# Even mixer of a ten-stage transformer kernel: C B products moved behind the x groups, output projection moved between scan units, bias mask made by matmul, products moved from GpSimd to VectorE

## The chip, the cores and the metric

The kernel runs on one core of one Trainium2 chip. The metric is the time of one execution on the device in microseconds. A core has TensorE (PE: matmuls, and the weight loads, PEld), VectorE (DVE), ScalarE (ACT), GpSimd (POOL) and SyncE (SP), each with a list of instructions of its own, run in order. They meet through semaphores. All constants, weights and inputs come from HBM by DMA.

## The reference, cut to what matters

x is 256 rows of 1024. It goes through ten stages: two macaron layers of feed-forward, mixer, feed-forward (stages a, conv, b, c, attn, d), then the even mixer, feed-forward e, the odd mixer and feed-forward f. Only the even mixer is touched:

```python
def even_mixer(x, ...):
    proj = rms_norm_2(x, mix_norm) @ w_in              # 1024 -> q, k, v (512 each), z (1024), xbc (2048), dt (32)
    q, k = rms_norm_2 of each head                     # 8 heads of 64
    na_out = neighbourhood_attention(q, k, v, rpb)     # 4 x 64 grid, window of 16 columns, relative bias
    xbc = silu(centred_depthwise_conv(xbc, conv_w, conv_b))   # 4 taps
    xs, bm, cm = split(xbc)                            # 1024, 512 (B), 512 (C)
    y = ssd_scan(forward) + ssd_scan(backward) + D_skip * xs  # 16 heads, 4 groups, chunks of 128
    ssd_out = gated_group_rms_norm(y, z, out_norm)
    return concatenate([na_out, ssd_out]) @ w_out      # 1536 -> 1024

# in neighbourhood_attention, for every row and head
s = q @ k * scale + bias[dy, dx]
s = where(in_win, s, -inf);  p = softmax(s);  o = p @ v

# in ssd_scan, for every chunk
y_diag = (C @ B^T * decay) @ (x * dt);   y_off = C @ h_prev * exp(a_cum)
```

## The kernel before, in words

The 256 rows are two tiles (t or l = 0, 1) of 128 partitions. Weights come as 260 pieces of 128 x 2048 f32, 1 MB each, in the order of use; SP loads them (`fetch`), ACT rounds a piece to f32r (`wh`, L1137), DVE makes the remainder (`wl`, L1752), and a product is three f32r matmuls: high by high, high by low, low by high. A loaded piece has 7 buffers (RAW), a rounded one 5 (RING). A piece p can only be rounded when p-5 has been used, and loaded when p-7 has been used. `ring.fill(most, done)` and `ring.need(upto)` in the lists of ACT and DVE say where in the list these splits stand. Both engines take them in order, so a split that waits for TensorE holds up everything behind it.

The even stage has 24 pieces, p0 = 160. On every engine its order is written out by hand as a list of calls, in `even()` of `tensor_program` (L835), `scalar_program` (L1440), `vector_program` (its `even`, with the list from L2259), `gpsimd_program` (L2466) and the load list in `sync_program`. The parts:

- `z_part`, then `group(0)` to `group(3)`: transposed projections of C, B and x. GROUPS = (2, 3, 0, 1), so groups 0 and 1 bring B and C, groups 2 and 3 bring x. ACT copies (`take`), DVE convolves (L2099), ACT applies silu (`gate`).
- `dt`: softplus on 64 columns over ACT and DVE (`steps_begin`, `step_exp`, `steps_middle`, `step_log`, `steps_end`); its result a2 (L2131) feeds `sums`, which yields the running sums and, through DVE's `sums`, the rows (L2145) for the decays.
- `state_products`: C B products of both tiles, banks 6, 7 and 2, 3.
- `qk_part`, `qk_turn`, `v_part`: q, k, v of the neighbourhood attention, with q's and k's norm: ACT squares, DVE `qk_sum`, POOL's root (L2439, L2442), DVE `qk_scale` (L2157, L2162, the latter makes qkg).
- the scan, in 8 units u of four heads (0 to 3 for tile 0): `decays(u)` builds the exponents of both directions in banks 2 and 3, ACT exponentiates (L1530), DVE `weigh(u)` multiplies (L2184), DVE `steps_x(u)` makes x dt (L2175), `outputs(u)` multiplies into banks 4 and 5. `crossing(l)` adds the state that crosses the chunks, from xe, which POOL's `entering(l)` makes (L2480). POOL's `skip` makes D x of tile 0 (L2489), DVE that of tile 1 (L2196). Then `skipped`, `gated` (L2207, L2210), ACT's `group_squares` (L1540), POOL's `group_root`, DVE's `normed` (L2219), and `turn_ssd` transposes the tile and splits it (L1547, L2226).
- the attention, in four pairs of heads i: SP's `nab_load(i)` (16 DMAs, L2588) brings the bias, reversed in each 64 columns; POOL's `nab_mask(i)` multiplies it by the window and adds -1e30 outside (L2503, L2505); TensorE `scores(i)`, DVE adds the bias (L2240) and takes the maximum (L2242), ACT exponentiates (L1555), DVE `divide(i)` (L2252), TensorE `turn(i, kk)` and `values(i)`.
- the output projection: pieces p0+18 to p0+21 for the scan (`out_ssd(q, t)`), p0+22 and p0+23 for the attention (`out_hood(q, t)`), 12 matmuls of 512 columns each, summed in banks 0 to 3. The `seam` adds it to x and scales for the next stage.

The whole output projection of tile 0 stands behind the last scan unit, `outputs(7)`.

## Time and profile before

| | before |
|---|---|
| median of 3 runs | 1761.22 us (1759.41 to 1762.1) |
| profiled execution | 1762.39 us, span 1761.1 us |
| PE busy | 1663.8 us, 94% |
| DVE busy | 981.4 us, 56% |
| ACT busy | 786.9 us, 45% |
| POOL busy | 100.2 us, 6% |
| mean granted TensorE clock | 0.968 |
| even stage, TensorE | about 1014 to 1261 us |

A row of a view of groups gives the line, the engine, the operation, what it writes and reads, the shapes and the count. In a view in order of time the first number is the start in us, the second the duration of the row (several instructions can be merged), and the bracket at the end the idle time before it with what ended it. PEclk is the granted clock in parts of 2.4 GHz. A busy PE is not PE at its peak: ends of matmuls are modelled, so unit costs are best taken between starts.

### The profile page before, as it was taken

The numbers are of one execution on the slowest core, as the hardware profiler recorded it, in microseconds if no ns is written. First come the engines' busy times: TensorE is split into PE (matmuls) and PEld (weight loads), VectorE is DVE, ScalarE is ACT, GpSimd is POOL, SyncE is SP. The second block draws the span as 40 slices with busy tenths as digits, with TensorE's granted clock in tenths as the row PEclk, the third lists the DMA queues.
The fourth block names the chain that finished last, engine by engine and source line by source line (L and its number), as shares of the span: only waits on it lengthen the run. The fifth ranks groups of instructions, "written<-read, shape, count | busy, mean of one in ns | idle before, by whom it ended". The sixth has DMA issues, their size and how long they took to land. (4 is left out here: it accounts for less than half of the span.)

```text
span 1761.1 us, 18639 instructions
## 1 busy us (share of the span) xinstructions
PE 1663.8 (94%) x7930; PEld 1357.7 (77%) x7930; DVE 981.4 (56%) x989; ACT 786.9 (45%) x953; POOL 100.2 (6%) x118
## 2 busy tenths in 40 slices
PE   6999998999999999989999998997899998599999
PEld 5877776788878888887888888775688886378887
DVE  4646675554474546665454556666545457644543
ACT  5444544444353434554343456433444444534442
POOL 1000100100010000001000000224000002000000
PEclk9999998999999999999999999977999999699999
DMA  8444541555455544543554453323365544025451
GB/s 325 186 185 174 191 156 48 193 189 191 169 190 193 200 184 178 197 166 120 191 195 187 176 194 122 119 61 88 127 220 186 191 185 153 1 96 218 188 191 48
DMA packets 51391, 289.36 MB, mean 164 GB/s; under 512 B 14023, under 2 KB 14791, under 8 KB 18026
## 3 DMA queue, kind: packets, MB, share of 16 engines
q1 hardware_dynamic: 50732, 286.87, 44.4%
q8 instruction: 63, 1.03, 0.2%
q10 hardware_dynamic: 576, 1.29, 0.2%
q14 instruction: 20, 0.16, 0.0%
HBM read 287.09 MB, written 1.05 MB: 164 GB/s over the span
## 5 line engine op out<-in xcount | busy, mean ns | idle before, releaser
L1752 DVE TENSOR_TENSOR wl<-raw,wh 128x2048 fp32r<-128x2048 f32 x260 | 588.8, 2286 | 177.9 <-ACT wh L1137 177.9
L513 PE MATMUL ps<-wh,xTh 128*128 128x512 f32 x1408 | 560.5, 398 | 20.1 <-DVE wl L1752 8.4
L513 PE MATMUL ps<-wh,xTl 128*128 128x512 f32 x1408 | 553.5, 393 | 0.0
L513 PE MATMUL ps<-wl,xTh 128*128 128x512 f32 x1408 | 553.2, 393 | 0.0
L1137 ACT ACTIVATE wh<-raw 128x2048 fp32r<-128x2048 f32 x260 | 489.0, 1907 | 2.7 <-PE ps L513 1.5
L513 PEld LDWEIGHTS ps<-wh,xTh 128*128 128x128 f32 x1408 | 267.6, 190 | 86.3 <-issue 10.1
L513 PEld LDWEIGHTS ps<-wh,xTl 128*128 128x128 f32 x1408 | 267.3, 190 | 57.3
L513 PEld LDWEIGHTS ps<-wl,xTh 128*128 128x128 f32 x1408 | 268.0, 190 | 54.1
L2439 POOL TENSOR_SCALAR st<-st 128x1 f32<-128x1 f32 (+2 forms) x46 | 30.3, 658 | 1452.7 <-ACT tmp L1156 850.5
L1200 ACT ACTIVATE sgf<-ps,st 128x256 f32<-128x256 f32 x22 | 10.5, 476 | 104.1 <-PE ps L513 104.1
L1200 ACT ACTIVATE sge<-ps,st 128x256 f32<-128x256 f32 x22 | 10.5, 476 | 99.5 <-PE ps L513 99.5
L513 PE MATMUL ps<-xTh,wh 128*128 128x256 f32 x192 | 54.7, 285 | 0.0
L513 PE MATMUL ps<-xTl,wh 128*128 128x256 f32 x192 | 54.3, 283 | 0.0
L513 PE MATMUL ps<-xTh,wl 128*128 128x256 f32 x192 | 54.3, 283 | 0.0
L1200 ACT ACTIVATE sgc<-ps,st 128x256 f32<-128x256 f32 x22 | 10.4, 474 | 96.0 <-PE ps L513 96.0
L1200 ACT ACTIVATE sgd<-ps,st 128x256 f32<-128x256 f32 x22 | 10.4, 475 | 95.6 <-PE ps L513 95.6
L1200 ACT ACTIVATE sgb<-ps,st 128x256 f32<-128x256 f32 x22 | 10.4, 474 | 93.0 <-PE ps L513 93.0
L1824 DVE SCALAR_TENSOR_TENSOR hbe<-ps,st,sge 128x256 f32<-128x256 f32 x22 | 10.6, 484 | 73.6 <-ACT sge L1200 73.5
L1824 DVE SCALAR_TENSOR_TENSOR hbf<-ps,st,sgf 128x256 f32<-128x256 f32 x22 | 10.6, 484 | 72.9 <-ACT sgf L1200 72.9
L1200 ACT ACTIVATE sga<-ps,st 128x256 f32<-128x256 f32 x22 | 10.5, 476 | 91.2 <-PE ps L513 91.2
L1824 DVE SCALAR_TENSOR_TENSOR hbc<-ps,st,sgc 128x256 f32<-128x256 f32 x22 | 10.6, 483 | 70.0 <-ACT sgc L1200 70.0
L1824 DVE SCALAR_TENSOR_TENSOR hbd<-ps,st,sgd 128x256 f32<-128x256 f32 x22 | 10.6, 483 | 69.7 <-ACT sgd L1200 69.7
(329 smaller groups left out, 2328.6 us busy)
## 6 DMA issues: line engine op xcount, KB each, us to landing
raw<-in_w SPq DMA_DIRECT2D x260, 1024.0 KB, 4.8
gains<-in_rows SPq DMA_DIRECT2D x18, 512.0 KB, 4.1
x<-in_x ACTq DMA_DIRECT2D x2, 512.0 KB, 8.4
qn<-in_rpb SPq DMA_DIRECT2D x32, 32.0 KB, 2.5
xd<-in_rpb SPq DMA_DIRECT2D x32, 32.0 KB, 2.6
out_x<-x SPq DMA_DIRECT2D x2, 512.0 KB, 2.6
df<-in_cst SPq DMA_DIRECT2D x1, 368.0 KB, 23.4
tri<-in_cst SPq DMA_DIRECT2D x1, 320.0 KB, 6.1
```

What stands on the lines that cost most here:

```text
L513: return pe.matmul(o, lhs, rhs, start=start, stop=stop, skip_group_check=False)
L1137: act.activation(wh[:, p % RING, :], raw[:, p % RAW, :], ACT.Copy).then_inc(*hi(p))
L1200: act.activation(r.sg[:, j % 2, t, :], bank(ffn_bank(j, t))[:, 0:256], ACT.Silu, scale=stat(("r", name, t))).then_inc(*silu(f, j, t))
L1752: TT(wl[:, p % RAW, :], raw[:, p % RAW, :], wh[:, p % RING, :].bitcast(F32), ALU.subtract).then_inc(*lo(p))
L1824: STT(r.hb[:, j % 2, t, :], bank(ffn_bank(j, t))[:, 256:512], stat(("r", name, t)), r.sg[:, j % 2, t, :], ALU.mult, ALU.mult).then_inc(*pr ...
L2439: pool.tensor_scalar(v, ss, mul, add, ALU.mult, ALU.add).then_inc(*mean(*name))
```

## The change

- Window mask: the constant `win` is only 0 or -1e30, ACT makes an f32r copy `winr`, and `scores` begins each bank with one matmul identity x winr of 512 columns, onto which q k is summed. DVE's addition reads the raw bias reversed. POOL's `nab_mask` is gone.
- Bias blocks: four semaphores; block 0 goes to qn, 1 and 2 to the two halves of nab, 3 to xd. nab_load(1) waits for decays(7), nab_load(3) for outputs(7), block 2 for nothing of its own. fetch(184) stands ahead of nab_load(0).
- `entering` and the skip product of tile 0 go from POOL to DVE.
- `sums` stands in the middle of `group(3)` (`mid`), not ahead of the products; `state_products` is split by tile, in banks 4, 5 and 2, 3, and stands behind group(3) and around qk_part(0, 0); the x turns and qk_turn(0, 0) come later, `crossing(0)` behind `outputs(0)`.
- `turn_ssd(0)` uses banks 6 and 7 and stands behind outputs(5); out_ssd(0..3, 0) stand between the units 7, the scores and the last outputs. turn(3, 1) uses bank 6. The tail's turns, values and out_hood are regrouped; out_hood(1, 0) stands inside out_ssd(3, 1).
- The lists of ACT and DVE follow, with many splits at other places.

```diff
@@ -855,15 +860,15 @@
         m.then_inc(*formed("sums"))
         emptied[2], emptied[3] = [(made, "dec")], [(made, "sums_lo")]
 
-    def state_products():
+    def state_products(t):
         on.wait_ge(silu, "xc", 3)
-        for t, b in ((0, 6), (1, 2)):
-            clear(b, b + 1)
-            for g in range(4):
-                m = mm(bank(b + g // 2)[:, 256 * (g % 2):256 * (g % 2) + 256], ev.xc[:, 8 + g, 128 * t:128 * t + 128],
-                       ev.xc[:, 12 + g, :], True, True)
-            m.then_inc(*formed("cb", t))
-            emptied[b] = emptied[b + 1] = [(copied, "cb", t)]
+        b = 2 if t else 4
+        clear(b, b + 1)
+        for g in range(4):
+            m = mm(bank(b + g // 2)[:, 256 * (g % 2):256 * (g % 2) + 256], ev.xc[:, 8 + g, 128 * t:128 * t + 128],
+                   ev.xc[:, 12 + g, :], True, True)
+        m.then_inc(*formed("cb", t))
+        emptied[b] = emptied[b + 1] = [(copied, "cb", t)]
 
     def qk_part(j, t):
         project("evenmix", p0 + 12 + 2 * j, t, 6 + t, (made, "qk", j, t))
...
@@ -923,30 +928,34 @@
 
     def turn_ssd(l):
         on.wait_ge(made, "ssd_out", l)
+        b0 = 2 if l else 6
         for b in range(2):
-            clear(2 + b)
-            transposes(2 + b, [xn[:, l, 512 * b + 128 * k:512 * b + 128 * k + 128] for k in range(4)]).then_inc(*flipped("ssd", l, b))
-            emptied[2 + b] = [(act_lo, "ssd", l, b)]
+            clear(b0 + b)
+            transposes(b0 + b, [xn[:, l, 512 * b + 128 * k:512 * b + 128 * k + 128] for k in range(4)]).then_inc(*flipped("ssd", l, b))
+            emptied[b0 + b] = [(act_lo, "ssd", l, b)]
 
     def scores(i):
         clear(6, 7)
         on.wait_ge(copied, "qk", 1, 1)
-        for t in range(2):
-            for hh in range(2):
-                u = slice(64 * hh, 64 * hh + 64)
-                m = mm(bank(6 + hh)[:, 256 * t:256 * t + 256], ev.qTn[u, i, 128 * t:128 * t + 128], ev.kTn[u, i, :], True, True)
+        on.wait_ge(copied, "win")
+        for hh in range(2):
+            mm(bank(6 + hh), ev.trir[:, 0, :], spread(ev.winr[:, :], 1, 8), True, False)
+            u = slice(64 * hh, 64 * hh + 64)
+            for t in range(2):
+                m = mm(bank(6 + hh)[:, 256 * t:256 * t + 256], ev.qTn[u, i, 128 * t:128 * t + 128], ev.kTn[u, i, :], False, t == 1)
         m.then_inc(*scored("hood", i))
         emptied[6] = emptied[7] = [(weighed, "hood", i, 1)]
 
     def turn(i, kk):
         on.wait_ge(made, "hood", i)
-        clear(4)
+        b = hood_bank(i, kk)
+        clear(b)
         for hh in range(2):
             for t in range(2):
-                m = pe.transpose(bank(4)[:, 256 * hh + 128 * t:256 * hh + 128 * t + 128],
+                m = pe.transpose(bank(b)[:, 256 * hh + 128 * t:256 * hh + 128 * t + 128],
                                  hood_P(i)[:, t, hh, 128 * kk:128 * kk + 128], ident[:, :])
         m.then_inc(*turned("hood", i, kk))
-        emptied[4] = [(copied, "hood", i, kk)]
+        emptied[b] = [(copied, "hood", i, kk)]
 
     def values(i):
         clear(5)
...
@@ -986,20 +995,20 @@
     emptied[3] = [(made, "dt")]
     group(1)
     group(2)
-    sums()
-    state_products()
-    group(3)
+    group(3, sums)
+    state_products(0)
     qk_part(0, 0)
+    state_products(1)
     x_turn(0)
     qk_part(0, 1)
+    x_turn(1)
     decays(0)
-    x_turn(1)
-    qk_turn(0, 0, 4)
+    qk_turn(0, 0, 5)
     qk_part(1, 0)
     decays(1)
     qk_turn(0, 1, 5)
+    outputs(0)
     crossing(0)
-    outputs(0)
     qk_part(1, 1)
     decays(2)
     outputs(1)
...
@@ -1016,38 +1025,37 @@
     outputs(4)
     decays(6)
     outputs(5)
+    turn_ssd(0)
+    out_ssd(0, 0)
     decays(7)
     outputs(6)
+    out_ssd(1, 0)
     scores(0)
     outputs(7)
-    turn_ssd(0)
-    out_ssd(0, 0)
+    out_ssd(2, 0)
     scores(1)
-    out_ssd(1, 0)
+    out_ssd(3, 0)
     turn(0, 0)
-    out_ssd(2, 0)
     turn(0, 1)
     scores(2)
-    out_ssd(3, 0)
     turn_ssd(1)
+    values(0)
     turn(1, 0)
-    values(0)
     out_ssd(0, 1)
     turn(1, 1)
     scores(3)
     out_ssd(1, 1)
+    values(1)
     turn(2, 0)
-    values(1)
+    turn(2, 1)
+    out_hood(0, 0)
+    values(2)
+    turn(3, 0)
+    turn(3, 1)
     out_ssd(2, 1)
-    turn(2, 1)
-    out_ssd(3, 1)
-    turn(3, 0)
-    values(2)
-    out_hood(0, 0)
-    turn(3, 1)
+    values(3)
+    out_ssd(3, 1, lambda: out_hood(1, 0))
     out_hood(0, 1)
-    values(3)
-    out_hood(1, 0)
     turn_in(AFTER["even"], 0)
     out_hood(1, 1)
 
...
     ring.need(p0 + 6)
@@ -1592,44 +1600,44 @@
     take(0, 1)
     gate(0, 0)
     ring.need(p0 + 8)
-    ring.fill(1, p0 + 6)
+    ring.fill(2, p0 + 6)
+    gate(0, 1)
     take(1, 0)
-    gate(0, 1)
-    step_exp()
-    ring.fill(1, p0 + 6)
     take(1, 1)
-    step_log()
     gate(1, 0)
     ring.need(p0 + 10)
     ring.fill(1, p0 + 8)
+    step_exp()
     take(2, 0)
+    step_log()
     gate(1, 1)
     ring.fill(1, p0 + 8)
     take(2, 1)
-    sums()
     gate(2, 0)
-    sum_rows()
-    state_products()
     ring.need(p0 + 12)
     ring.fill(1, p0 + 10)
+    gate(2, 1)
...
@@ -2166,6 +2173,11 @@
         TT(ev.dte[:, 1, :], d3[0][:, 0, 0:16], ev.dec[:, 2, :], ALU.mult)
         TT(ev.dte[:, 0, :], d3[0][:, 1, 16:32], ev.dec[:, 3, :], ALU.mult).then_inc(*made("dte"))
 
+    def entering(l):
+        on.wait_ge(copied, "xs", 1 - l, 1)
+        on.wait_ge(made, "dte")
+        TT(xe_of(l).rearrange("p (h d) -> p h d", d=64), heads(xn[:, 1 - l, :]), spread(ev.dte[:, l, :], 2, 64), ALU.mult).then_inc(*made("xe", l))
+
     def steps_x(u):
         l, q = u // 4, u % 4
         on.wait_ge(copied, "xs", l, q // 2)
...
@@ -2236,8 +2246,11 @@
             on.wait_ge(formed, "off", 1)
         for t in range(2):
             S = bank(6, 2).rearrange("p (h t n) -> p h t n", h=2, t=2)[:, :, t, :]
-            on.wait_ge(pooled, "nab", i, t)
-            TT(P[:, t, :, :], B[:, t, :, :], S, ALU.add).then_inc(*weighed("hood", i, t))
+            on.wait_ge(nab_in[i], i)
+            Bt = B[:, t, :, :]
+            rev = bass.AP(tensor=Bt.tensor, offset=Bt.offset + 63, ap=[list(Bt.ap[0]), [256, 2], [64, 4], [-1, 64]])
+            TT(P[:, t, :, :].rearrange("p h (j c) -> p h j c", c=64), rev, S.rearrange("p h (j c) -> p h j c", c=64),
+               ALU.add).then_inc(*weighed("hood", i, t))
             on.wait_ge(weighed, "hood", i, t)
             dve.tensor_reduce(ev.sm[:, a + 6 * t:a + 6 * t + 2], P[:, t, :, :], AX.X, ALU.max, negate=True).then_inc(*peaked("hood", i, t))
 
...
@@ -2264,63 +2277,63 @@
     turn_in("evenmix", 1)
     ring.fill(1, p0)
     key_gain()
-    ring.fill(1, p0 + 2)
-    ring.fill(1, p0 + 4)
+    ring.fill(2, p0 + 2)
     ring.need(p0 + 6)
     ring.fill(2, p0 + 4)
     convolve(0, 0)
-    ring.need(p0 + 8)
-    ring.fill(1, p0 + 6)
     convolve(0, 1)
     steps_begin()
-    ring.fill(1, p0 + 6)
+    ring.need(p0 + 8)
+    ring.fill(2, p0 + 6)
     convolve(1, 0)
-    steps_middle()
+    convolve(1, 1)
     ring.need(p0 + 10)
     ring.fill(1, p0 + 8)
-    convolve(1, 1)
+    steps_middle()
+    convolve(2, 0)
     steps_end()
     ring.fill(1, p0 + 8)
-    convolve(2, 0)
-    sums()
+    convolve(2, 1)
     ring.need(p0 + 12)
     ring.fill(1, p0 + 10)
-    convolve(2, 1)
+    convolve(3, 0)
+    sums()
     ring.fill(1, p0 + 10)
-    convolve(3, 0)
+    convolve(3, 1)
     ring.need(p0 + 14)
     ring.fill(1, p0 + 12)
-    convolve(3, 1)
     qk_sum(0, 0)
     factors()
     steps_x(0)
+    qk_scale(0, 0)
     ring.fill(1, p0 + 12)
-    qk_scale(0, 0)
     qk_sum(0, 1)
+    steps_x(1)
     weigh(0)
+    qk_scale(0, 1)
     ring.need(p0 + 16)
-    qk_scale(0, 1)
-    steps_x(1)
-    ring.fill(1, p0 + 12)
+    entering(0)
+    ring.fill(1, p0 + 13)
     qk_sum(1, 0)
     weigh(1)
     qk_scale(1, 0)
+    entering(1)
+    ring.fill(1, p0 + 14)
     crossed(0)
-    ring.fill(1, p0 + 14)
     steps_x(2)
     qk_sum(1, 1)
     weigh(2)
     ring.need(p0 + 18)
     qk_scale(1, 1)
-    ring.fill(1, p0 + 14)
+    ring.fill(1, p0 + 15)
     steps_x(3)
     weigh(3)
     ring.fill(1, p0 + 16)
+    skipped(0)
     steps_x(4)
-    skipped(0)
     weigh(4)
+    ring.fill(1, p0 + 17)
     gated(0)
-    ring.fill(1, p0 + 16)
     crossed(1)
     steps_x(5)
     weigh(5)
...
@@ -2328,14 +2341,13 @@
     steps_x(6)
     weigh(6)
     ring.fill(1, p0 + 18)
+    turn_ssd(0)
     steps_x(7)
     weigh(7)
     ring.need(p0 + 22)
+    scores(0)
     skipped(1)
-    turn_ssd(0)
     gated(1)
-    scores(0)
-    ring.fill(1, p0 + 18)
     scores(1)
     divide(0)
     normed(1)
...
@@ -2473,53 +2485,16 @@
         on.wait_ge(peaked, "qk", j, t)
         root(("qk", j, t), stat(("ss", "qk", j, t), 8), mul, add, 8)
 
-    def entering(l):
-        on.wait_ge(copied, "xs", 1 - l, 1)
-        on.wait_ge(made, "dte")
-        on.wait_ge(formed, "cb", 1)
-        pool.tensor_tensor(xe_of(l).rearrange("p (h d) -> p h d", d=64), xn[:, 1 - l, :].rearrange("p (h d) -> p h d", d=64),
-                           spread(ev.dte[:, l, :], 2, 64), ALU.mult).then_inc(*pooled("xe", l))
-
-    def skip():
-        Dk = small[:, SMALL["dskip"][0]:SMALL["dskip"][0] + 16]
-        x3 = xn[:, 0, :].rearrange("p (h d) -> p h d", d=64)
-        on.wait_ge(made, "xd", 3)
-        on.wait_ge(pooled, "xe", 1)
-        on.wait_ge(small_in_)
-        pool.tensor_tensor(x3, x3, spread(Dk, 2, 64), ALU.mult).then_inc(*pooled("xk"))
-
-    def nab_mask(i):
-        raw_in = hood_raw(i)
-        on.wait_ge(nab_in[i % 2], i)
-        on.wait_ge(const_in["win"])
-        if i < 2:
-            on.wait_ge(formed, "decay", 7, 1)
-        else:
-            on.wait_ge(weighed, "hood", i - 2, 1)
-        for t in range(2):
-            B = raw_in[:, t, :, :]
-            rev = bass.AP(tensor=B.tensor, offset=B.offset + 63, ap=[list(B.ap[0]), [64, 8], [-1, 64]])
-            N8 = hood_bias(i)[:, t, :, :].rearrange("p h (j c) -> p (h j) c", c=64)
-            pool.tensor_tensor(N8, rev, spread(ev.win[:, 0, :], 1, 8), ALU.mult).then_inc(*pooled("nab_in", i, t))
-            on.wait_ge(pooled, "nab_in", i, t)
-            pool.tensor_tensor(N8, N8, spread(ev.win[:, 1, :], 1, 8), ALU.add).then_inc(*pooled("nab", i, t))
-
     def group_root(l):
         on.wait_ge(squared, "ssd", l)
         root(("ssd", l), stat(("ssd", l), 4), 1.0 / 256, 1e-6, 4)
 
     qk_root(0, 0)
     qk_root(0, 1)
-    entering(0)
     qk_root(1, 0)
-    entering(1)
     qk_root(1, 1)
-    skip()
     group_root(0)
-    nab_mask(0)
     group_root(1)
-    for i in range(1, 4):
-        nab_mask(i)
     seam("even")
 
...
@@ -2577,15 +2552,15 @@
     if i == 0:
         on.wait_ge(flipped, "qk", 1, 1)
     elif i == 1:
+        on.wait_ge(formed, "decay", 7, 1)
+    elif i == 3:
         on.wait_ge(formed, "out", 7)
-    else:
-        on.wait_ge(pooled, "nab", i - 2, 1)
-    dst = hood_raw(i)
+    dst = hood_bias(i)
     for r in range(4):
         for j in range(4):
             off = 2 * i * 465 + (j - r + 7) * 31 - 48
             src = bass.AP(tensor=rpb_in.tensor, offset=off, ap=[[1, 64], [465, 2], [1, 64]])
...
```

## Rows read from the trace of the kernel before

**Rows 1.** Stretches: us, busy of PE, PEld, DVE, ACT, POOL (count), PEclk, DMA share, GB/s

```profile
1125.00:1165.00 40.00, 39.31 (x200) 30.07 (x198) 22.09 (x27) 15.69 (x19) 8.18 (x6) 1.00 0.08 27
1165.00:1190.00 25.00, 23.67 (x98) 18.02 (x97) 19.63 (x25) 8.64 (x18) 9.45 (x6) 0.62 0.37 108
...
1210.00:1262.00 52.00, 45.36 (x219) 34.25 (x220) 33.68 (x45) 24.25 (x42) 11.22 (x10) 0.92 0.41 132
```

**Rows 2.** TensorE in order of time: start, us, operation, count, idle before

```profile
1079.97 1.86 PE L513 MATMUL ps<-dz,tri 128*128 128x16 f32 x8 [3.86 <-DVE act L2131]
...
1088.17 0.47 PE L513 MATMUL ps<-xTh,wh 128*128 128x256 f32 x1
...
1099.87 0.40 PE L513 MATMUL ps<-wh,xTh 128*128 128x512 f32 x1
...
1119.13 1.12 PE L522 MATMUL ps<-ident,qn 128*128 128x128 f32 x4 [4.30 <-DVE qn L2162]
...
1126.91 0.40 PE L513 MATMUL ps<-trir 128*128 128x512 f32 x1
...
1158.58 0.40 PE L513 MATMUL ps<-trir 128*128 128x512 f32 x1
...
1160.62 2.00 PE L513 MATMUL ps<-xd,xc 128*128 128x64 f32 x16
1162.45 1.95 PE L513 MATMUL ps<-xc,cbm 128*128 128x256 f32 x8
...
1190.08 0.79 PE L513 MATMUL ps<-wh,xTh 128*128 128x512 f32 x1 [1.41 <-DVE xTl L2226]
...
1195.15 1.13 PE L513 MATMUL ps<-kTn,qTn 64*128 64x256 f32 x8
...
1245.13 0.48 PE L513 MATMUL ps<-wh,oTh 128*128 128x512 f32 x1
...
1248.11 1.08 PE L513 MATMUL ps<-cbm,vn 128*64 128x256 f32 x8
...
1261.52 0.39 PE L513 MATMUL ps<-wh,xTh 128*128 128x512 f32 x1
```

**Rows 3.** Waits of TensorE in the even stage: total, times, longest

```profile
PE ps L946 <- DVE xc L2252: 10.6, 1, 10.6
```

**Rows 4.** TensorE by single microseconds: us, busy (count), PEclk, DMA share, GB/s

```profile
1123.00:1124.00 1.00, 1.00 (x6) 0.99 0.00 0
...
1170.00:1171.00 1.00, 1.00 (x6) 0.90 0.39 44
...
1194.00:1195.00 1.00, 1.00 (x4) 0.65 0.24 45
```

**Rows 5.** DVE in order of time, and one line's durations: min/median/max ns

```profile
1163.91 1.22 DVE L2210 TENSOR_TENSOR xn<-xn,zs 128x1024 f32<-128x1024 f32 x1
...
1171.24 1.67 DVE L2219 SCALAR_TENSOR_TENSOR xn<-xn,st,gains 128x256 f32<-128x256 f32 x4 [0.90 <-POOL st L2442]
1172.83 0.75 DVE L2175 TENSOR_TENSOR xd<-xn,dz 128x256 f32<-128x256 f32 x2
1173.50 1.28 DVE L2184 TENSOR_TENSOR xc<-xc,cbm 128x512 f32<-128x512 f32 x2
1174.70 2.28 DVE L1752 TENSOR_TENSOR wl<-raw,wh 128x2048 fp32r<-128x2048 f32 x1
...
L2252 DVE TENSOR_SCALAR xc<-xc,smn x16: 345/352/1441, 1208.5 to 1238.9; 128x256 f32<-128x256 f32 x16
```

**Rows 6.** SP's queue in order of time, and the page's issues: count, KB, us to landing

```profile
1197.90 10.35 SPq L2588 DMA_DIRECT2D qn<-in_rpb  x16
...
qn<-in_rpb SPq DMA_DIRECT2D x32, 32.0 KB, 2.5
```

**Rows 7.** The mask's second product on POOL: count, min/median/max ns, first and last start

```profile
L2505 POOL TENSOR_TENSOR nab<-nab,win x8: 1261/1286/2128, 1179.5 to 1224.5; 128x512 f32<-128x512 f32 x8
```

**Rows 8.** Two lines of the rope on DVE: count, min/median/max ns

```profile
L2380 DVE TENSOR_TENSOR r<-qg,gcs x4: 692/692/694, 1468.0 to 1504.3; 128x512 f32<-128x512 f32 x4
...
L2381 DVE TENSOR_TENSOR r<-qg,gcs x4: 682/684/685, 1468.6 to 1504.9; 128x512 f32<-128x512 f32 x4
```

108 lines of the change are left out of this document (56 added, 52 removed).

## Prediction

> **What bounds the kernel now.** I read the page first: TensorE is busy for nine tenths of the span, so time comes off only where it idles or runs at half clock. The change touches only the even stage, so the next view is busy time by stretch [rows 1], where PEclk 1.00 is the 2.4 GHz level and 0.50 the 1.2 GHz level: the stretch from 1125 to 1165 us is full, the one from 1165 to 1190 is recorded as busy but at a mean grant of 0.62, and 1210 to 1262 has 6.6 us of gaps. Then TensorE's instructions in order of time [rows 2], whose brackets give each wait: 3.9 us ahead of sums for a2, 4.3 us ahead of qk_turn(0,0) for qkg, and in the view of waits the longest of the stage, 10.6 us for DVE's divide [rows 3]. Behind that last one stands POOL: DVE's scores wait for nab, the masked bias (L2505) [rows 7], and POOL waits for its load, which SP issues block after block [rows 6]. Feed-forward "e" starts its first matmul at 1261.52 [rows 2], and from there TensorE waits for nobody up to the next mixer, so a shift of that start moves the end by as much. I use the profiled execution: span 1761.1 us, 1.3 around it, 1762.4 in all; the median of the runs is 1.2 us lower.
>
> **Unit costs at full clock**, from starts in [rows 2]: a two-unit decay build (decays) 1160.62-1158.58 = 2.0 us, outputs 1162.45-1160.62 = 1.8, crossing 1.8, an out-projection piece (12 matmuls) 1248.11-1245.13 = 3.0 with a short pause, so 2.9. A group (transposed projection) takes 1099.87-1088.17 = 11.7. A plain projection, twice the matmuls of an out-projection piece at a slightly shorter pace, 5.4. Turns of four blocks take 0.5, values 1.1, scores 1.0. At half clock the same out-projection piece took 1195.15-1190.08 = 5.1, so 2.2 more.
>
> **Part 1, the front (sums inside group(3), C B products after it, qk and x turns later).** Before, sums waits 3.9 us for a2, then products wait 0.7, both with an engine clocked down: 1079.97 to 1086.1 is 6.1 us for work of 3.0 (sums 1.2, one product 1.8), 3 us lost. Then qk_turn(0,0) waits 4.3 us and it and the projection behind it take 1126.91-1119.13 = 7.8 us instead of 5.9, 1.9 lost. Sum: 3.9+0.7+4.3+3.0+1.9 = 13.8 us. What is late next? I walked the new lists with the unit costs. The second weight piece of group(3) is cast by ACT at 1068.3 and its low part is made by DVE at 1070.7 (two splits now follow group(0), instead of one and one), and group(2) ends at 1075.9: 5 us to spare. steps_middle follows at 1070.7, ACT's logarithm at 1073.0, convolve(2,0) lies between, and a2 is made at 1075.3; sums now stands half way into group(3) and asks at 1081.6: 6 us. factors needs ACT's exponential of dec, now behind state_products(1), at 1100.3; after it steps_x(0) and qk_scale(0,0) make qkg at 1103.0, and its turn, now behind two x turns and decays(0), asks at 1107: 4 us. entering(0) on DVE is done at 1110.9 and crossing asks at 1117.4: 6 us; weigh(0) at 1108.3 and outputs(0) at 1115.6: 7 us. So the gain is taken whole: v_part(0) starts at 1128.6, not at the 1142.3 of before (1128.6 is also what the unit costs give, added from 1075.9). If that cover is gone, the 3.9 and the 4.3 come back.
>
> **Part 2, products off POOL.** POOL loses two entering, the skip product and sixteen bias products, the additions among them 1.26 to 2.1 us [rows 7]. DVE gains two entering and one skip product: 1.2 us each, as L2210, which multiplies two tiles of the same shape [rows 5]; at least 1.2 and, from the worst case of a product stretched beside POOL in [rows 5] (1441 for 345 ns), at most four times that, which needs POOL at work there; I take 1.2. On the way DVE's own instructions get their normal length back: one TENSOR_SCALAR of divide ran from 345 to 1441 ns [rows 5], the long ones where POOL worked. The reversed read of the bias moves to DVE: the same kind of read in the rope (L2380) takes 692 ns against 684 for the plain one (L2381) [rows 8], so 0 to 0.1 us in all. The mask costs TensorE two matmuls of 512 columns per scores: 4 x 2 x 0.23 = 1.9 us, bounds 0, where all lies beside waits, and 3.4 at half clock. I count 0.5 in each scores on the walk below.
>
> **Part 3, the scan's second half.** Here DVE becomes the bound. From 1141.0 (wh of piece p0+20 ready) its list holds, by starts as in [rows 5]: split 2.2, skip 2.4, steps_x and weigh 1.9, split 2.2, gated 2.4, crossed 1.15, steps_x and weigh 1.9, normed 1.6, steps_x and weigh 1.9, split 2.2, turn_ssd(0) 1.3, together 21.2; and it waits 1.1 for wh and 0.9 for the group root. So xTl of tile 0 is ready at 1164.1, while TensorE has ended turn_ssd(0) at 1159.8: a new wait of 4.3 us ahead of out_ssd(0,0). And the clock: v_part(1) ended at 1158.6, only scan units followed, and the grant fell at 1170.9 with TensorE recorded as busy throughout; it rose at 1194.6, 4.6 us into the first dense piece [rows 2, 4]. In the new order v_part(1) ends at 1144.0 and the same kind of work follows, so I let it fall at about 1156 and rise near 1169: out_ssd(0,0) costs 5.1. What the low clock costs before 1164 is hidden by DVE. From 1169.2: decays(7) 2.0, outputs(6) 1.85, out_ssd(1,0) 2.9, scores(0) 1.5, outputs(7) 1.85, out_ssd(2,0) 2.9, scores(1) 1.5, out_ssd(3,0) 2.9, end 1186.6.
>
> The Trainium skill (TensorE: Matmul & The Clock Gate, "What's actually happening") has the gate follow how busy TensorE has been. Read simply, a busy stretch would then keep the clock, and rival B below would be the result; the fall in [rows 4] without idle time speaks against that reading.
>
> **Part 4, the tail.** DVE from scores(0) at 1177.6: scores 2.7, skip 2.4, gated 2.4, scores(1) 2.7, divide 1.4, so turn(0,0) at 1189.3 (wait 2.7, instead of 10.6). Now bias: SP issues 16 DMAs in 10.4 us, landing 2.5 us later [rows 6]. Block 0 is issued from 1150 behind both fetches. Blocks 1 and 2 wait for decays(7), 1171.2, and land at 1184 and 1194.5. Queued behind them on SP are block 3 and fetch(191), the weights of "e", issued from 1202 and needed at 1218: no cost. scores(2) on DVE waits for block 2 to 1194.5 and takes 2.7; ACT's exponentials and DVE's remainders take 2.9 more (as the step from the last maximum to xTl took before), so out_ssd(0,1) starts at 1200.3 after a wait of 5.2. The old wait of 4.3 us brought half clock from within it until 1123.0, 3.9 us after the restart at 1119.13 [rows 2, 4], so this piece costs 5.1 again, end 1205.4. turn(1,1), scores(3), out_ssd(1,1), values(1), turn(2,0): 6.5, to 1211.9. turn(2,1) needs ACT's copy, which stands behind split 1.9+2.2, scores(3) 2.7, exponentials 1.1, oTh 0.4, table 1.4, copy 0.6 from 1206.5: 1217.0, wait 5.1. out_hood(0,0) at half clock, to 1222.6; values(2) and two turns 2.1; out_ssd(2,1) 2.9, values(3) 1.1, half of out_ssd(3,1) 1.45, to 1230.1. out_hood(1,0) waits for values(3) behind a split that asks for out_ssd(2,1): 1232.3, wait 2.2. Then 2.9+1.45+2.9+1.0+2.9 = 11.1: "e" starts at 1243.4. The old wait for xn ahead of turn_in is covered by out_hood(0,1) and half a piece.
>
> **Sum.** 1261.5-1243.4 = 18.1 us: 13.8 in the front, 4.3 behind it, where three half-clock pieces and five waits take the place of old ones. 1762.4-18.1 = 1744.3 for a profiled execution, 1743.1 as a median.
>
> **Rivals.**
> A, the forecast: 1743. For it: every step has a row, and DVE's chain to 1164 adds up without gaps.
> B, the clock holds. The out-projection now stands among the last scan units instead of behind them all; if the grant then stays at 1.00 throughout, three times 2.2 us fall away: 1736.5. Against it stand the falls in [rows 1]; for it, that the tail of before held 0.92 in spite of its gaps.
> C, the tail stays slow. If the low grant of 1156 lasts as it did before (24 us), until about 1181, four pieces and three scan units go at half clock, some 9 us more, of which the nab and DVE waits absorb some 2: 1750. Or the front keeps one of its waits: 1748 to 1752.
> D, the other side: TensorE at 1.2 GHz from 1156 to the end of the stage, because waits on DVE, bias and copies come every few us. The tail holds 58 us of full-clock matmul work; at 5.1 for 2.9 that is 44 more than full clock, less 7 already counted and some 14 that now fill waits: 23 us against a gain of 18, so 1766. It decides once about 50 us of that work are slow. Against it: 1210 to 1262 had such gaps at a mean grant of 0.92 [rows 1].
> E, it doesn't do what it says: POOL's products were hidden, DVE loses elsewhere what POOL gave, and only the front counts at half: 1754 to 1760. Little speaks for it, since DVE waits on nab by name.
>
> **Chances.** A 0.50, B 0.15, C 0.22, E 0.06, D 0.04, and 0.03 for no change by other ways. The range, 1735 to 1754, takes in A to C but for the ends of each. About 0.2% (3.5 us) is what a measurement of this kernel can tell from no change: faster is A to C and two thirds of E, 0.91; the rest of E and the 0.03 are same, 0.05; slower is D, 0.04.
>
> **What would show it.** Right: no wait for a2 or qkg; v_part(0) near 1129; DVE nearly gapless from 1141 to 1164, and TensorE waiting for xTl at L2226's successor ahead of out_ssd(0,0); PEclk 0.5 around 1157 to 1169; scores(2) waiting for the bias DMA; "e" starting near 1243. Wrong: a wait inside group(3) for a split, L2240's successor well above 0.69 us, or a long low PEclk behind 1170.

## The result and the profile after

The changed kernel takes 1748.83 us in the median (1745.70 to 1750.12, 4 runs), the kernel before 1760.32 (1759.28 to 1762.10, 4 runs): ratio 0.9927, 95% interval 0.9915 to 0.9939. It is faster, by 11.5 us where I had forecast 18.1. The time lies inside the range and 5.7 us above its centre. The profiled execution took 1749.03 us, its span is 1747.6 against 1761.1, and "e" starts at 1248.13 instead of 1261.52 [rows 2]: 13.4 of the 13.5 us of the span come from the even stage. A difference between two kernels is read from these ratios; where it is under some 3 us, their intervals mostly overlap and it stays unproven.

The page of the kernel after, its span and busy time by engine:

```profile
span 1747.6 us, 18630 instructions
PE 1664.8 (95%) x7938; PEld 1356.6 (78%) x7938; DVE 974.7 (56%) x992; ACT 786.6 (45%) x954; POOL 69.3 (4%) x99
```

Its view of TensorE's waits in the even stage (1040 to 1262 us): total, times, longest:

```profile
PE ps L516 <- DVE xTl L2236: 7.3, 2, 4.2
PE ps L955 <- ACT cbm L1574: 4.2, 2, 3.5
PE ps L516 <- DVE oTl L2270: 2.1, 1, 2.1
PE ps L955 <- DVE xc L2265: 1.4, 1, 1.4
```

The waits for a2 and qkg are gone, and the 10.6 us for the divide [rows 3] are 1.4 (now DVE xc L2265). In their place stand five waits of 14.3 us in sum. TensorE in order of time (start, duration, operation, idle before):

```profile
1157.62 1.97 PE L516 MATMUL ps<-xd,xc 128*128 128x64 f32 x16 [0.28 <-DVE xc L2196]
1160.10 1.09 PE L525 MATMUL ps<-ident,xn 128*128 128x128 f32 x8 [0.52 <-DVE xn L2229]
1165.37 0.80 PE L516 MATMUL ps<-wh,xTh 128*128 128x512 f32 x1 [4.18 <-DVE xTl L2236]
...
1179.09 0.40 PE L516 MATMUL ps<-winr,trir 128*128 128x512 f32 x1
1179.41 1.13 PE L516 MATMUL ps<-kTn,qTn 64*128 64x256 f32 x4
1180.47 0.50 PE L516 MATMUL ps<-winr,trir 128*128 128x512 f32 x1
1180.90 1.13 PE L516 MATMUL ps<-kTn,qTn 64*128 64x256 f32 x4
...
1193.90 0.66 PE L955 MATMUL ps<-ident,xc 128*128 128x128 f32 x4 [1.40 <-DVE xc L2265]
...
1204.42 0.50 PE L516 MATMUL ps<-wh,xTh 128*128 128x512 f32 x1 [3.12 <-DVE xTl L2236]
...
1220.29 1.11 PE L955 MATMUL ps<-ident,xc 128*128 128x128 f32 x4 [3.51 <-ACT cbm L1574]
...
1235.70 0.68 PE L516 MATMUL ps<-wh,oTh 128*128 128x512 f32 x1 [2.11 <-DVE oTl L2270]
```

The 4.18 is the new wait of Part 3, ahead of out_ssd(0,0). The four rows at 1179 are one scores: two mask matmuls, and after each the two q.k matmuls of one head; with the next instruction at 1181.95 it takes 2.86 us. The clock by single stretches (us, busy of PE, PEld, DVE, ACT, POOL, PEclk, DMA share, GB/s):

```profile
1162.00:1164.00 2.00, 0.00 (x0) 0.00 (x0) 2.00 (x1) 0.00 (x0) 0.00 (x0) 1.00 0.19 38
1164.00:1165.00 1.00, 0.00 (x0) 0.00 (x0) 1.00 (x3) 0.00 (x0) 0.00 (x0) 0.59 0.00 0
...
1171.00:1172.00 1.00, 1.00 (x4) 0.48 (x3) 0.00 (x0) 0.11 (x1) 0.00 (x0) 1.00 0.00 0
1174.00:1175.00 1.00, 1.00 (x9) 1.00 (x8) 0.28 (x1) 0.00 (x0) 0.00 (x0) 0.71 0.18 33
1175.00:1176.00 1.00, 1.00 (x4) 0.81 (x4) 0.00 (x0) 0.00 (x0) 0.00 (x0) 0.50 0.23 45
```

The grant falls inside the idle stretch, at 1164.2, is back at 1171.0, and falls a second time at 1174.4 (0.71 is the mean of that microsecond) with TensorE recorded as busy. DVE ahead of the wait (start, duration, idle before):

```profile
1149.78 2.29 DVE L1759 TENSOR_TENSOR wl<-raw,wh 128x2048 fp32r<-128x2048 f32 x1 [1.11 <-ACT wh L1145]
...
1158.37 1.67 DVE L2229 SCALAR_TENSOR_TENSOR xn<-xn,st,gains 128x256 f32<-128x256 f32 x4 [0.90 <-POOL st L2454]
1159.96 0.76 DVE L2187 TENSOR_TENSOR xd<-xn,dz 128x256 f32<-128x256 f32 x2
1160.63 1.28 DVE L2196 TENSOR_TENSOR xc<-xc,cbm 128x512 f32<-128x512 f32 x2
1161.84 2.28 DVE L1759 TENSOR_TENSOR wl<-raw,wh 128x2048 fp32r<-128x2048 f32 x1
1164.04 1.28 DVE L2236 TENSOR_TENSOR xTl<-ps,xTh 128x512 fp32r<-128x512 f32 x2
```

What out_ssd(0,0) waits for stands in DVE's queue behind steps_x(6), weigh(6) and a weight split, 4.1 us of work that it doesn't need. Not all of it is wait: TensorE's transposes and ACT's copy, which it does need, end only inside this time.

### The profile page after: what moved, and what is told of

Same layout as the page of the kernel before. It is cut to its first block and busy times, and to the rows that moved or that the text cites. A ratio compares the mean times of both kernels' runs of the same rounds, so it can differ in the third digit from the quotient of the medians.

```text
span 1747.6 us, 18630 instructions
## 1 busy us (share of the span) xinstructions
PE 1664.8 (95%) x7938; PEld 1356.6 (78%) x7938; DVE 974.7 (56%) x992; ACT 786.6 (45%) x954; POOL 69.3 (4%) x99
## 5 line engine op out<-in xcount | busy, mean ns | idle before, releaser
L516 PE MATMUL ps<-xTh,wh 128*128 128x256 f32 x192 | 54.6, 284 | 0.0
L1831 DVE SCALAR_TENSOR_TENSOR hbe<-ps,st,sge 128x256 f32<-128x256 f32 x22 | 10.6, 483 | 73.4 <-ACT sge L1208 73.4
L1831 DVE SCALAR_TENSOR_TENSOR hbf<-ps,st,sgf 128x256 f32<-128x256 f32 x22 | 10.6, 483 | 72.8 <-ACT sgf L1208 72.8
L1831 DVE SCALAR_TENSOR_TENSOR hbd<-ps,st,sgd 128x256 f32<-128x256 f32 x22 | 10.6, 483 | 71.3 <-ACT sgd L1208 71.3
L1831 DVE SCALAR_TENSOR_TENSOR hbc<-ps,st,sgc 128x256 f32<-128x256 f32 x22 | 10.6, 484 | 69.7 <-ACT sgc L1208 69.7
```

Source lines behind the costliest of these rows:

```text
L516: return pe.matmul(o, lhs, rhs, start=start, stop=stop, skip_group_check=False)
L1831: STT(r.hb[:, j % 2, t, :], bank(ffn_bank(j, t))[:, 256:512], stat(("r", name, t)), r.sg[:, j % 2, t, :], ALU.mult, ALU.mult).then_inc(*pr ...
```

## The experiments

Two measures are given for each kernel: the ratio to the kernel before on the same chip, and the length of the even stage in the profiled execution, from the first matmul of group(0) to turn_in of tile 1 for "e": before 1269.68-1040.96 = 228.7 us, after 1256.42-1041.50 = 214.9. The stage leaves out what the clock does elsewhere: in the 490 us behind it, the grant is at 0.50 for 31 to 34 us, at changing places, and the executions of the kernel with paired scores alone lie between 1744.3, at a mean clock of 0.977, and 1749.1. Being of one execution, the stage carries the clock of its own. This table gives it, from each profile: the first fall of the grant in the second half of the stage, counted from the first matmul of group(0), and the time at 0.50 in the whole stage.

| kernel | stage, us | first fall, us from group(0) | at 0.50, us |
|---|---|---|---|
| before | 228.7 | 129.9 | 54.6 |
| before, q.k head by head | 224.1 | 139.8 | 37.5 |
| the front alone | 217.3 | 119.1 | 41.0 |
| the front and one line of SP | 215.0 | 116.3 | 41.0 |
| after | 214.9 | 122.7 | 23.9 |
| products back on GpSimd | 214.9 | 122.6 | 23.9 |
| masks first, heads outside | 211.7 | 122.6 | 23.9 |
| paired scores | 211.6 | 119.1 | 27.3 |
| paired scores, no mask | 212.0 | 116.3 | 34.1 |
| idle matmuls in the new wait | 211.7 | 116.2 | 17.1 |
| output projection put back | 211.1 | 119.1 | 30.7 |
| DVE's order | 208.4 | 116.4 | 20.5 |
| the tail in order | 199.6 | 116.5 | 17.1 |
| the last kernel | 192.5 | 143.1 | 6.8 |

The kernels made from the one after have the same list on TensorE up to outputs(5), which ends some 118 us from group(0). Their first fall lies at 116, 119 or 122.6 us all the same, but for the last kernel. So a part of each difference in the stage belongs to the execution and not to the edit. The second row shows how much: its kernel doesn't differ from the one before ahead of the first scores, its grant falls 9.9 us later, and its stage is 4.6 us shorter with no change in time. A stage difference of up to 5 us is therefore a hint at most, unless the clock columns agree; one of 10 is not in doubt.

**The front alone** (the kernel before with the new orders of group(3), products, x turns and qk turns on TensorE, ACT and DVE; the rest as it was):

```diff
-                sums()
-                state_products()
-                group(3)
+                group(3, sums)
+                state_products(0)
                 qk_part(0, 0)
+                state_products(1)
                 x_turn(0)
...
```

> The kernel before with the front of the change alone: sums inside group(3), products of C and B by tile behind it, x turns and qk_turn(0,0) later, the splits of ACT and DVE as in the change up to the end of the scan. entering, skip and the bias mask stay on POOL, and everything from turn_ssd(0) on is as before. Forecast by the prediction's sum: 13.8 us, so about 1746.5 against 1760.3, with v_part(0) starting near 1129. Rival (the front's gain is eaten by the tail, since DVE and the bias set the tail): v_part(0) near 1129 all the same, but wait for divide longer than 10.6 us, total gain under 8 us.

1755.80 us, ratio 0.9966 [0.9955, 0.9978]; stage 217.3. The gain is 6.2 us, not 13.8, so the forecast failed; the rival had the size, but not the reason, since the wait for the divide got shorter (9.1), not longer. The front's own gain is there: counted from group(0), the decays ahead of v_part(0) start at 83.6 us here and in the kernel after, and the waits for a2 and qkg are gone. But it is given back in part. TensorE, ACT, DVE and SP's queue of this kernel:

```profile
1173.92 3.64 PE L513 MATMUL ps<-xd,xc 128*128 128x64 f32 x16 [5.49 <-DVE xc L2184]
```

```profile
1167.66 1.91 ACT L1139 ACTIVATE wh<-raw 128x2048 fp32r<-128x2048 f32 x1 [9.12 <-DMA raw<-in_w]
...
1169.61 2.29 DVE L1752 TENSOR_TENSOR wl<-raw,wh 128x2048 fp32r<-128x2048 f32 x1 [7.12 <-ACT wh L1139]
```

```profile
1152.07 10.47 SPq L2586 DMA_DIRECT2D qn<-in_rpb  x16
1162.58 1.07 SPq L2557 DMA_DIRECT2D raw<-in_w  x2
```

Two weight pieces stand behind the 16 issues of the first bias block; ACT waits 9.1 us for their data, DVE 7.1 for ACT, and outputs(7) waits 5.5 us for the weigh behind that split.

**The front and one line of SP:**

```diff
-            fetch(182)
-            nab_load(0)
             fetch(184)
+            nab_load(0)
```

> The kernel with the front part alone (x groups ahead of C B on TensorE, ScalarE and VectorE; GpSimd products, scores, mask and output projection as before; 1755.8 us, 0.9966), plus the one line moved on the SP queue: the fetch of chunk 184 stands ahead of the 16 issues of the first bias block. Theory Q (the front's gain was partly given back because the weights' halves came late behind the 10.5 us of bias issues, seen as 5.5 us of outputs(7) waiting for weigh): that wait falls under 1 us, the even stage gets 3 to 5 us shorter than the 217.3 of the front alone, and the time comes to 1751 to 1753 (ratio 0.994 to 0.995). Rival R (the 5.5 us was the chain of VectorE and would move to the next wait, the divide's or turn_ssd's): the wait for weigh goes, the divide wait grows from 9.1 by the same, the time stays within 0.1% of 1755.8.

1750.87 us, ratio 0.9935 [0.9918, 0.9952]; stage 215.0. The wait for weigh is gone and the divide's wait stays (9.1, now 9.3): theory Q by the waits and by the time (4.9 us, 5.5 by the ratios); the stage got 2.3 us shorter, less than the 3 to 5 expected. More important: the front with this line has all of the change's gain that can be measured (0.9935 against 0.9927, intervals almost the same, and stages of 215.0 and 214.9). What the mask, the products and the interleaved output projection bring together, in the form they have, is 1.4 us by the two ratios, which is inside their intervals.

**The scores.** Three kernels take the 2.86 us apart. From the kernel before, q.k head by head:

```diff
-                    for t in range(2):
-                        for hh in range(2):
-                            u = slice(64 * hh, 64 * hh + 64)
+                    for hh in range(2):
+                        u = slice(64 * hh, 64 * hh + 64)
+                        for t in range(2):
```

> The kernel before with one edit: the four q k matmuls of scores(i) with the head outside and the tile inside. No mask matmul. Theory S: each scores takes 2.1 us instead of 1.1, at full clock; most of it lies ahead of waits for DVE there, so 0 to 3 us more in all. Theory M: 1.1 us stays and the time is that of before.

1760.04 us, ratio 0.9991 [0.9982, 1.0001], no change; the stage of its profile is 224.1, 4.6 shorter, with 17 us less of it at half clock. That isn't the edit's doing, as said above. From the kernel after, both masks first and the heads inside:

```diff
                     for hh in range(2):
                         mm(bank(6 + hh), ev.trir[:, 0, :], spread(ev.winr[:, :], 1, 8), True, False)
-                        u = slice(64 * hh, 64 * hh + 64)
-                        for t in range(2):
+                    for t in range(2):
+                        for hh in range(2):
+                            u = slice(64 * hh, 64 * hh + 64)
```

> The changed kernel with one edit: in scores(i) both mask matmuls come first, then the four q k matmuls with the tile outside and the head inside, as before the change, so that neighbours use partitions 0 to 63 and 64 to 127 in turn. Same work. Theory S (order): a scores took 1.1 us for its four q k matmuls before and 2.1 us after (1179.41 to 1180.47 is one head), because two neighbours on the same 64 partitions no longer overlap. Then each scores takes 1.8 us instead of 2.86, and up to four times 1.0 us come off the even stage: about 1745 instead of 1748.8. Theory M (mixing): the q k matmuls are slow because they add to a bank begun by an f32r matmul. Then the order changes nothing: 2.86 us stays and the time is 1748 to 1750.

1747.97 us, ratio 0.9924 [0.9909, 0.9938]; stage 211.6, 3.3 shorter. It changes two things, so a third kernel moves the masks ahead and leaves the heads outside:

> The changed kernel with one edit: both mask matmuls of a scores stand ahead of the four q.k matmuls, whose order stays head by head as in the changed kernel. Before, the four q.k took 1.07 us with the heads inside and 1.07 with the heads outside; in the changed kernel, where a mask matmul on all 128 rows stands between the two heads, each head's two take 1.07. Theory T (the matmul on all 128 rows between the heads keeps the two halves of the array from working side by side; the order of the heads costs nothing): a scores takes 1.62 us as with the paired order, the stage 211 to 213, time 1747 to 1748. Rival H (accumulating onto the mask makes the order of the heads count): a scores takes 2.5 to 2.9 us, stage 214 to 216, time 1748 to 1750.

1749.38 us, ratio 0.9930 [0.9913, 0.9947]; stage 211.7. A scores in the kernel before with the heads outside (first fence), and in this last one:

```profile
1179.23 1.14 PE L513 MATMUL ps<-kTn,qTn 64*128 64x256 f32 x8
```

```profile
1180.44 0.63 PE L516 MATMUL ps<-winr,trir 128*128 128x512 f32 x2
1181.00 1.14 PE L516 MATMUL ps<-kTn,qTn 64*128 64x256 f32 x8
1182.07 2.00 PE L516 MATMUL ps<-xd,xc 128*128 128x64 f32 x16
```

Four q.k matmuls take 1.07 us in either order of the heads; with a mask matmul of 128 rows between the heads, two take 1.07. So theory T holds: the order of the heads costs nothing, the matmul between them costs 1.2 us a scores (2.86 against 1.63). The single records of the traces show why. One q.k matmul is two records, so a row of eight has four of each head. In the kernel after the four of one head start one by one, at 1179.41, 1179.73, 1179.95 and 1180.17 us, and then comes the mask of the other head. In this last kernel the eight start in pairs 0.01 us apart, 1181.00 and 1181.01, then 1181.32 and 1181.33, and so on: the two heads, whose operands lie on different 64 rows, run side by side, although they stand one behind the other in the list. Both kernels gain 3.3 us in the stage; the last one has the same clock columns as the kernel after, so its 3.3 us are the edit's. The ratios show nothing of it: behind the stage both took 493.4 us instead of 491.2, with the clock's falls in the odd mixer at other places. Whether these two belong together stayed open.

**No mask** (the paired kernel without the two mask matmuls; it leaves the window of the attention out):

> The changed kernel with scores in the paired order and without the two mask matmuls of each scores (the window of the neighbourhood attention is left out, so this kernel computes another attention). It prices the mask on TensorE. With the pair and the mask a scores took 1.62 us; without it the q.k alone should take 1.07 to 1.13. Theory: the two matmuls of 512 columns cost what they take, 0.5 to 0.6 us a scores where TensorE is the bound, four times 2.2 us at most: stage 209.4 to 211, time 1745.8 to 1747.5 (paired with mask: 1748.0). Rival: the scores stand ahead of waits on VectorE and ScalarE which then take up the time won, stage 211.6 as before, time within 0.1% of 1748.0. The 1.9 us (bounds 0 to 3.4) that the prediction had for the mask would be right in the first case and too much in the second.

1744.95 us, ratio 0.9908 [0.9892, 0.9925]; stage 212.0, not shorter than the 211.6 with the mask. A scores takes 1.07 us, and the waits behind it grow (divide 2.7 to 3.1, ACT's copy 4.7 to 5.2), as the rival has it. But this execution had 6.8 us more at half clock than the one with the mask, the median is 3.0 lower, below both forecasts, and the intervals overlap. What the mask costs in time stays open.

**Idle matmuls in the new wait** (16 more on the way to out_ssd(0,0), their result unused):

```diff
                 turn_ssd(0)
+                clear(2)
+                for _ in range(16):
+                    mm(bank(2), ev.trir[:, 0, :], spread(ev.trir[:, 1, :], 1, 4), True, True)
                 out_ssd(0, 0)
```

> The changed kernel with 16 idle matmuls (identity by mask, 512 columns, 3.7 us at full clock, result thrown away) behind turn_ssd(0), where TensorE waits 4.2 us for xTl. Theory K (the grant falls because TensorE stands still there, and half clock then costs 2.2 us in out_ssd(0,0) and 1.3 us by the second fall at 1174.7): PEclk stays 1.00 up to about 1180, out_ssd(0,0) takes 2.9 instead of 5.3 us, 3 to 4 us off, about 1745. Rival (the clock falls by the scan units alone, as at 1170.9 before without any idle time): it falls all the same near 1165 to 1175, and the time stays within 1 us of 1748.8 or grows by what the fillers add at half clock.

1744.85 us, ratio 0.9918 [0.9901, 0.9935]; stage 211.7. The gap is filled, and out_ssd(0,0) runs at full clock. TensorE, and DVE's row that makes what the piece waits for:

```profile
1161.23 4.79 PE L516 MATMUL ps<-trir 128*128 128x512 f32 x16
1165.86 0.39 PE L516 MATMUL ps<-wh,xTh 128*128 128x512 f32 x1
...
1168.63 0.40 PE L516 MATMUL ps<-trir 128*128 128x512 f32 x1
```

```profile
1162.68 1.28 DVE L2239 TENSOR_TENSOR xTl<-ps,xTh 128x512 fp32r<-128x512 f32 x2
```

The piece takes 2.8 us instead of 5.3, and no second fall comes at 1174. The grant had fallen at 1156.3 here, ahead of the idle matmuls, and came back at 1163.1, under them; in the kernel without the mask, where it fell at the same place and TensorE waited 2.6 us, it came back at 1169.7. So the idle matmuls brought the clock back earlier. They have a price: xTl was ready at 1164.0 and the piece starts at 1165.9, because the idle matmuls, in part at half clock, run 1.9 us over. The net gain isn't shown: 3.2 us in the stage of an execution with a different clock, and a ratio inside the interval of the kernel after. Theory K had the clock at 1.00 up to 1180, which it was not.

**The output projection put back** (turn_ssd(0) and out_ssd(q,0) behind outputs(7) on all engines, banks 2 and 3; from the kernel after):

```diff
-                turn_ssd(0)
-                out_ssd(0, 0)
                 decays(7)
                 outputs(6)
-                out_ssd(1, 0)
                 scores(0)
                 outputs(7)
-                out_ssd(2, 0)
+                turn_ssd(0)
+                out_ssd(0, 0)
                 scores(1)
-                out_ssd(3, 0)
+                out_ssd(1, 0)
...
```

> The changed kernel with the first tile's output projection put back to where it stood: turn_ssd(0) and out_ssd(0..3, 0) behind outputs(7), between the scores and the turns, in banks 2 and 3. Front, mask by matmul and products on VectorE stay. Theory P (the projection between the scan units is what covers VectorE's chain there): the 4.2 us wait for xTl goes from its place, but outputs(6), outputs(7) and scores(0) then wait for VectorE's weighs (2 to 5 us each), and the even stage is 3 to 8 us longer than the 214.9 of the changed kernel, time 1752 to 1757. Rival N (TensorE's and VectorE's totals set it, order inside the scan's end doesn't matter): the waits only change places, stage 214 to 216, time within 0.1% of 1748.8.

1744.89 us, ratio 0.9905 [0.9890, 0.9920]; stage 211.1. Both theories missed: undoing this part doesn't make the kernel slower. It is faster by 3.8 us in the stage and in the ratios by as much, with intervals that overlap a little. The waits for VectorE that I feared for outputs(6) and outputs(7) didn't come: from 1160 to 1178 decays(7), outputs(6), scores(0) and outputs(7) ran at half clock without a pause, slow enough for DVE to keep up, and in this stretch one wait of 1.4 us, for xTl, is left. In the kernel after, TensorE stands still in a part of the same time.

**DVE's order** (from the kernel after; the same move on ACT):

```diff
                 steps_x(6)
+                turn_ssd(0)
                 weigh(6)
                 ring.fill(1, p0 + 18)
-                turn_ssd(0)
```

> The changed kernel with turn_ssd(0) of VectorE moved ahead of weigh(6) and the split behind it (both engines). Theory V (what out_ssd(0,0) waits for is VectorE's queue order: the split and weigh(6), 3.6 and 1.2 us, stand ahead of the copies it needs): the 4.2 us wait for xTl falls to 0 to 1 us, TensorE's clock does not fall at 1165, and the stage is 3 to 5 us shorter than 214.9, time 1744 to 1746. Rival W (weigh(6) late now holds outputs(6), a unit later): a wait of 3 to 5 us for weigh(6) or weigh(7) takes its place, time within 0.1% of 1748.8.

1743.22 us, ratio 0.9901 [0.9876, 0.9926]; stage 208.4. The wait is 1.4, not 4.2, and nobody is late for weigh(6), as theory V has it. But the wait mixes two things. Counted from group(0), out_ssd(0,0) starts at 122.6 us instead of 123.9, so the order brings it forward by 1.2 us. The rest of the 2.8 is TensorE, which comes to the wait later, at half clock: in the kernel without the mask, with the old order and the same first fall, the wait is 2.6 us and the piece starts at 123.9. The wait for xTl of tile 1 is shorter too, 1.0 instead of 3.1. The stage is 6.5 us shorter, with another clock; the ratio's interval overlaps that of the kernel after. Whether the projection is better between the scan units (this kernel) or behind them (the one above) isn't settled: 2.7 us by the stage, 0.7 by the ratios, both inside what the clock alone can do.

**Products back on GpSimd** (two entering and the first skip):

> The changed kernel with the three products (two entering, the first skip) back on GpSimd, where each took 1.9 us against 1.22 on VectorE. Theory: of VectorE's gapless chain from 1141.4 to turn_ssd(0) at 1164.0 the skip's 1.2 us goes, the two entering products lay in slack; so the wait for xTl falls from 4.2 to about 3.0 and the time by 1.2, at most 2.8 us with the clock held a little longer: 1746 to 1747.6. Rival (the prediction's place for the new wait is wrong, the chain is held by ScalarE's weight copies ahead of the splits): the wait stays at 4.2 and the time within 0.1% of 1748.8.

1750.46 us, ratio 0.9931 [0.9916, 0.9945]; stage 214.9 with the same clock columns, the wait 4.2 as before: the rival. DVE is busy 2.0 us less from 1040 to 1160, and its split still starts when ACT's wh is there:

```profile
1150.07 2.29 DVE L1759 TENSOR_TENSOR wl<-raw,wh 128x2048 fp32r<-128x2048 f32 x1 [1.10 <-ACT wh L1145]
```

**The tail in order.** From the kernel after: paired scores; the move above; turn_ssd(1) ahead of scores(2) on ACT and DVE; ACT's turns of block 2 ahead of a weight cast and the table load; scores(3) and values(3) ahead of their splits.

```diff
...
                 turn(0, 1)
-                scores(2)
                 turn_ssd(1)
                 turn(1, 0)
                 values(0)
+                scores(2)
                 turn(1, 1)
...
```

> The changed kernel with scores in the paired order, turn_ssd(0) ahead of weigh(6), turn_ssd(1) ahead of scores(2) on ScalarE and VectorE, the turns of block 2 ahead of the split and the table load on ScalarE, scores(3) and values(3) ahead of their splits. If the five waits of the tail (4.2, 3.1, 1.4, 3.5, 2.1 us) were each an order of a queue and nothing else: all under 1 us, scores 1.6 each instead of 2.9, half-clock stretches fewer; the stage 10 to 16 us shorter than 214.9 and the time 1733 to 1739 (ratio 0.983 to 0.987). Rival: VectorE is the bound of the whole tail, and each microsecond taken from one wait comes back in the next (the divide's or the splits for the next stage); then the stage gets only 3 to 5 us shorter, as with the paired scores alone (1748.0) and with idle matmuls in the first wait (1744.9), 1743 to 1746.

1736.16 us, ratio 0.9856 [0.9839, 0.9872]; stage 199.6, 15.3 shorter: the orders of the queues, as forecast, and clear of the interval of the kernel after. Not all five waits went under 1 us; the divide's is 2.7 and ACT's copy 3.0. Here SP's bias block does bind, DVE's scores(3) waiting for its landing:

```profile
1204.42 0.69 DVE L2253 TENSOR_TENSOR xc<-xd,ps 128x512 f32<-128x512 f32 x1 [3.36 <-DMA xd<-in_rpb]
```

The second block waits for decays(7), which the change put behind out_ssd(0,0). So the last kernel has two moves more, decays(7) between turn_ssd(0) and out_ssd(0,0) and divide(0) ahead of scores(1) on DVE:

```diff
                 turn_ssd(0)
-                out_ssd(0, 0)
                 decays(7)
+                out_ssd(0, 0)
                 outputs(6)
```

> The last version (paired scores, VectorE's and ScalarE's orders of the tail; 1736.2 us, 0.9856; even stage 199.6) with two more moves of one line each: decays(7) on TensorE between turn_ssd(0) and out_ssd(0,0), and divide(0) on VectorE ahead of scores(1). Theory: decays(7)'s 2.0 us cover the 1.4 us wait for xTl, and they let the SP queue start the second bias block at about 1163 instead of 1169.7, so that the fourth block lands by 1199 and VectorE's 3.4 us wait for it, with TensorE's 3.0 us wait for the copy behind it, goes to about 0.5; the divide's wait of 2.7 falls under 1. In sum 1.4 + 1.7 + 2.5 = 5.6 us and some half-clock matmuls: stage 192 to 195, time 1729 to 1732 (ratio 0.981 to 0.983). Rival: decays(7) and the divide are late for someone else (weigh(7), scores(1) of VectorE), or the clock gives it back; then 1734 to 1737.

1731.30 us, ratio 0.9822 [0.9805, 0.9840]; stage 192.5. It beats both kernels, by 31 and by some 18 us. Its longest waits, where the longest lies, and its SP queue:

```profile
PE ps L956 <- ACT cbm L1575: 4.3, 2, 3.6
PE ps L516 <- DVE oTl L2271: 0.9, 1, 0.9
PE ps L516 <- ACT kTn L1525: 0.7, 1, 0.7
```

```profile
1185.86 1.11 PE L956 MATMUL ps<-ident,xc 128*128 128x128 f32 x4 [3.58 <-ACT cbm L1575]
```

```profile
1163.38 21.64 SPq L2564 DMA_DIRECT2D nab<-in_rpb  x32
1185.07 10.35 SPq L2564 DMA_DIRECT2D xd<-in_rpb  x16
```

The blocks start at 1163.4 instead of 1173.0, and DVE's scores wait for no bias. The waits for xTl and for the divide are gone. Time and stage are as forecast, one wait is not: in the divide's place TensorE waits 3.6 us for ACT's copy of the first turn, which stands in ACT's queue behind the exponentials of scores(1). The only fall of the grant in this stage, at 1184.8, lies in that wait.

## Why the prediction was right, and where its size was off

**The front** held as worked out: v_part(0) starts at 1128.90 (forecast 1128.6), and no wait came in the place of the two removed. Against the 1142.3 of before that is 13.4 us, and 13.9 counted from group(0), for 13.8 worked out.

**One edit wasn't priced.** I put fetch(184) ahead of the first bias block at nothing ("block 0 is issued from 1150 behind both fetches"). It was worth 4.9 us of time and 2.3 of stage; without it the front would have lost a part of its gain to outputs(7). It didn't make the number wrong, since I walked the tail with it in place.

**The new wait** of Part 3 was forecast at 4.3 and is 4.18, at its place. The reason I gave was half wrong. I had DVE bound from 1141.0 and counted the skip product into its chain; the chain really hangs on ACT's wh at 1149.8, where DVE waits 1.1, and on the group root at 1158.4. The skip's 1.2 us lie in that first gap, and putting it back on GpSimd changed nothing. That the order of DVE's queue has a part in it I had not seen: with turn_ssd(0) ahead of weigh(6) and the split, the piece starts 1.2 us earlier.

**Where the 4.7 us are.** "e" starts at 1248.1, not 1243.4. TensorE comes to turn(0,0) at 1192.5 instead of 1186.6, 5.9 us late. The term that was mis-sized is "scores 1.5": it measured 2.86, twice ahead of turn(0,0), 2.7 us. I had added two mask matmuls to the q.k of before and not asked what stands between the heads. The chain of DVE ended at 1165.3 instead of 1164.1, 1.2. The second fall of the clock at 1174.4, which I had not reckoned with, made outputs(6) and out_ssd(1,0) slower: 2.0 and 4.2 us instead of 1.85 and 2.9, about 1.5. The late return at 1171.0 added 0.4 to out_ssd(0,0) and decays(7). Then the terms trade: the wait ahead of turn(0,0) is 1.4 instead of 2.7, the one for xTl of tile 1 3.1 instead of 5.2, ACT's copy 3.5 instead of 5.1, the last 2.1 instead of 2.2, and at 1235.7 the lag is 3.4. A further low stretch from 1236 to 1239, on out_hood(1,0), makes it 4.7. The tail was to bring 4.3 us beyond the front and brought nothing. That the sum stayed this near is in part luck: four waits came out shorter than forecast, by 5.1 us in sum, and hid that much of what the scores, DVE's chain and the clock had added.

**The clock** fell within the new wait, at 1164.2, not at 1156. The grant came back 5.7 us after the restart. The second fall at 1174.4 had no idle time ahead of it but 3.4 us of busy rows at full clock. In four variants of this kernel the first fall came at 1156 to 1157, as I had put it, under the scan units with 0.3 us of idle time, and ahead of what the edits changed there. So whether it falls at 1156 or 1164 changes from execution to execution, and that one forecast place came true in some of them is luck as much as the miss here is. That the new wait brings the fall isn't shown: three profiles with the 4.2 us wait have their first fall in it, and the last kernel, without a wait there, none until 1184.8, but that kernel differs in more. Rival B, the clock that holds throughout, is refuted in every profile; the last kernel comes nearest.

The Trainium skill (TensorE: Matmul & The Clock Gate, "What's actually happening") has the gate follow how busy TensorE has been; the fall at 1164.2 and the early return under idle matmuls, at 1163.1, agree with it, the falls at 1156 to 1157 and 1174.4, read by busy time alone, don't.

**The bias load** was to hold scores(2) up to 1194.5. TensorE was itself later than that, so it didn't show; it showed as soon as the rest was quick.

**The mask** at 1.9 us of matmuls was near the size on TensorE (0.55 a scores). What it costs in time isn't settled, as said with the kernel without it; the break between the heads, 1.2 us a scores, was the larger price on TensorE.
